# A two-layer hybrid backbone with expert routing: last layer's gate applied as the expert outputs leave PSUM, three-term sum on TensorE, and routing tables of 28 turns

## The reference

```python
p_group = softmax(t @ w_router_group); grp = argmax(p_group)          # 4 groups
top_p, top_j = top_k(softmax(logits of that group's 8 experts), 2)
gates = gate_group * top_p / top_p.sum()
f[token] = sum over its 2 experts e of  gate * ((silu(h @ w_gate[e]) * (h @ w_up[e])) @ w_down[e])
x = layer_norm(RES_ALPHA * x + g2 * f, ln2_g, ln2_b)                  # g2: one value per channel
```

## Time and profile before

| | us |
|---|---|
| median of 3 runs | 2641.17 |
| the profiled execution | 2639.44 |
| its span, first to last instruction | 2637.6 |
| TensorE matmul busy | 2328.2 (88%) |
| VectorE busy | 942.3 (36%) |
| ScalarE busy | 445.2 (17%) |
| GpSimd busy | 483.1 (18%) |

### The profile page before, as it was taken

How to read it: one execution, slowest core, us unless ns; L and a number is a source line. 1 busy time by engine, 2 the same in 40 slices (tenths; PEclk the granted TensorE clock), 3 DMA queues, 4 the chain that set the end, 5 groups by cost and what they waited for, 6 DMA issues and landing times. The chain is left out here.

```text
span 2637.6 us, 38801 instructions
## 1 busy us (share of the span) xinstructions
PE 2328.2 (88%) x14940; PEld 1620.1 (61%) x14940; DVE 942.3 (36%) x2263; ACT 445.2 (17%) x1115; POOL 483.1 (18%) x615
## 2 busy tenths in 40 slices
PE   5999779997399999999949987999399999999975
PEld 3999645654366666666629984555166666666642
DVE  1777736565511101110126665566611011101107
ACT  0011123331011111111111113232011111111111
POOL 0000013444011111111111111344011111111114
PEclk8999879998599999999979998999699999999987
DMA  9555430001588999999841113000289999999944
GB/s 356 186 169 161 146 112 16 18 24 49 204 321 353 387 397 390 386 392 403 324 162 68 49 49 130 16 25 17 110 347 388 394 385 394 385 386 381 372 189 192
DMA packets 131278, 608.71 MB, mean 231 GB/s; under 512 B 21376, under 2 KB 24448, under 8 KB 112752
## 3 DMA queue, kind: packets, MB, share of 16 engines
q1 hardware_dynamic: 113168, 569.61, 55.9%
q0 software_dynamic: 16864, 37.78, 3.8%
q10 hardware_dynamic: 1152, 0.03, 0.0%
HBM read 599.41 MB, written 42.04 MB: 243 GB/s over the span
## 5 line engine op out<-in xcount | busy, mean ns | idle before, releaser
L1966 PEld LDWEIGHTS gate_up<-room,w_gate_up 128*128 128x128 f32 x4608 | 520.8, 193 | 31.5 <-issue 31.5
L1966 PE MATMUL gate_up<-room,w_gate_up 128*128 128x128 f32 x4608 | 527.6, 277 | 3.1 <-DVE room L1873 3.1
L1975 PE MATMUL down<-w_down,room 128*128 128x512 f32 x576 | 256.8, 599 | 0.0
L1983 PE MATMUL gate_up_short<-w_gate_up,room 128*64 128x512 f32 x1152 | 255.1, 595 | 0.0
L1882 DVE TENSOR_TENSOR room<-room,gate_up 128x128 f32<-128x128 f32 x144 | 41.4, 288 | 597.4 <-ACT room L1901 597.4
L1885 DVE TENSOR_TENSOR room<-room,gate_up_short 128x256 f32<-128x256 f32 x36 | 15.2, 421 | 495.0 <-ACT room L1907 495.0
L1983 PEld LDWEIGHTS gate_up_short<-w_gate_up,room 128*64 128x64 f32 x1152 | 79.5, 137 | 171.2 <-issue 171.2
L1975 PEld LDWEIGHTS down<-w_down,room 128*128 128x128 f32 x576 | 106.5, 190 | 123.0 <-issue 120.5
L1593 POOL COPY rows_idx<-slot_token 128x1 int32 (+1 forms) x78 | 14.3, 183 | 791.6 <-PE rows_turned L1953 710.6
L1996 PE MATMUL down<-w_down,room 128*64 128x512 f32 x576 | 131.5, 598 | 11.9 <-ACT room L1909 11.9
L1404 PE MATMUL proj<-w_out,mixT 128*128 128x512 f32 x288 | 129.5, 592 | 0.0
(11 more groups left out here) (365 smaller groups left out, 3254.8 us busy)
## 6 DMA issues: line engine op xcount, KB each, us to landing
w_gate_up<-in_w_exp_gate SPq DMA_DIRECT2D x72, 2048.0 KB, 9.2
w_gate_up<-in_w_exp_up SPq DMA_DIRECT2D x72, 2048.0 KB, 13.7
w_down<-in_w_exp_down SPq DMA_DIRECT2D x72, 2048.0 KB, 12.5
ada_w<-in_w_ada SPq DMA_DIRECT2D x96, 512.0 KB, 4.8
h_rows<-h SPq DMA_DIRECT2D x18, 512.0 KB, 2.6
w_out<-in_w_out SPq DMA_DIRECT2D x2, 4096.0 KB, 13.2
w_in<-in_w_in SPq DMA_DIRECT2D x2, 3072.0 KB, 17.4
xn<-expert_rows SPq DMA_DIRECT2D x10, 512.0 KB, 4.0
```

The costliest lines, as they stand in the source:

```text
L1966: mm = nc.tensor.matmul(H[j % 2][:, o, :], wgu[0][:, o, k, j * P:(j + 1) * P], xT[0][:, k, :], start=k == 0, stop=k == KT - 1)
L1975: mm = nc.tensor.matmul(Y[:, h, :], hid[:, j, :], wd[0][:, j, h * 512:(h + 1) * 512], start=j == 0, stop=j == JT - 1)
L1983: mm = nc.tensor.matmul(Hs[c * HP:(c + 1) * HP, :, :], xT[1][:, k, :], wgu[1][:, :, k, c * 2 * P:(c + 1) * 2 * P], start=k == 0, stop=k == ...
```

## The change

It has four parts.

1. **Last stage.** TensorE sums three terms in PSUM: alpha times x (a diagonal matrix of alpha, two matmuls per tile, ahead of the wait for the landing) and the two experts' rows times their gates (four). Three sums of two banks take turns. VectorE takes the statistics straight from PSUM, centres from PSUM, and does the multiplication with one over the deviation and the addition of the bias of the tile before in between. ScalarE and GpSimd do no 1024-wide work. The load of g2 is gone, and the norm's vectors are fetched between tiles 0 and 1.
2. **Last layer's loop.** g2 is applied as the outputs leave PSUM, by VectorE in place of ScalarE's copies; g2 is loaded at the start of the block, by three DMAs on SP's queue. The first layer's loop is as before.
3. **Counts.** `total` sums over the tiles in PSUM (N matmuls of 32 columns), `before` is completed for earlier tiles by N-1 more matmuls; the running sums on VectorE are gone. The lines are turned by five matmuls of one column. Comparisons over 320 or 256 elements become integer shifts.
4. **Tables.** 28 columns in place of 44. Empty slots are marked through an offset of the digits. Names are made while VectorE waits for the counts. Table and place instructions are interleaved, so that `table_ready` comes behind the one-hot tables. The long one-hot table comes in two halves, and the short slots are decoded first.

```diff
-NTURNS = 44
-NOWHERE = float(1 << 20)
+NTURNS = 28
+NO_NAME = 4096.0
...
+                if last:
+                    sp.dma_start(g2[:, :], g.mods[l, 0:1, 5 * D:6 * D].to_broadcast([P, D])).then_inc(g2_in, 16)
+                    for h in range(2):
+                        sp.dma_start(g2_s[h * HP:(h + 1) * HP, :], ...).then_inc(g2_in, 16)
                 each_turn(sp, weights)
...
-                step(nc.vector.tensor_copy(tot[:, :, :], r(total)))
-                for t in range(1, N):
-                    step(tt(tot[:, t, :], tot[:, t, :], tot[:, t - 1, :], ALU.add))
-                    done()
...
+                v.wait_ge(counted, 1)
+                step(ts(count_i[:, 0, :], total, float(P - 1), None, ALU.add))
+                step(ts(count_i[:, 1, :], total, float(HP - 1), None, ALU.add))
+                done()
+                step(ts(count_i[:, :, :], count_i[:, :, :], 7, None, ALU.arith_shift_right))
+                done()
+                step(tt(parts[:, SHORT, :], count_i[:, 0, :], count_i[:, 1, :], ALU.subtract))
+                step(nc.vector.tensor_copy(parts[:, LONG, :], count_i[:, 1, :]))
...
+                step(tt(turn_hot[:, :, :, :], iota(K_IOTA, TC), wide(bits_f[0], TC), ALU.is_equal))
...
+                tt(short_hot[:, :, :, :], iota(K_IOTA, HP), wide(bits_s, HP), ALU.is_equal).then_inc(slots_hot, 1)
...
                 for i in range(2):
                     tt(name_hot[:, :, :, i, :], turn_hot[:, :, :, :], over(digit[:, i, :, :], TC), ALU.mult).then_inc(slots_hot, 1)
+                v.wait_ge(s.sem, listed)
+                nc.vector.tensor_copy(tab[:, :], tab_f[:, :]).then_inc(table_ready, 1)
+                for h in range(2):
+                    t = slice(h * (N // 2), (h + 1) * (N // 2))
+                    tt(long_hot[:, t, :, :], ..., ALU.is_equal).then_inc(slots_hot, 1)
...
                     turn_copy(i, 1)
+                    if last:
+                        v.wait_ge(yo_free[0], i + 1)
+                        for h in range(2):
+                            v.wait_ge(y_full, i * 2 + h + 3)
+                            tt(yo[:, h * 512:(h + 1) * 512], Y[:, h, :], g2[:, h * 512:(h + 1) * 512], ALU.mult).then_inc(y_done, 1)
                     v.wait_ge(silu_s_done, i + 1)
                     nc.vector.tensor_tensor(hid_s[:, :], silu_s[:, :], Hs[:, 1, :], ALU.mult).then_inc(hid_s_done, 1)
                     turn_copy(i + 1, 0)
+                    if last:
+                        v.wait_ge(yo_free[1], i + 1)
+                        v.wait_ge(ys_full, i + 2)
+                        tt(yo_s[:, :], Y[:, 0, :], g2_s[:, :], ALU.mult).then_inc(ys_done, 1)
...
-                nc.tensor.matmul(total, g.k[:, K_ONE:K_ONE + P], m, start=True, stop=True).then_inc(counted, 1)
-                nc.tensor.matmul(before, g.k[:, K_TRI:K_TRI + P], m, start=True, stop=True).then_inc(prefixed, 1)
+                ones = g.k[:, K_ONE:K_ONE + P]
+                for t in range(N):
+                    mm = nc.tensor.matmul(total, ones, both[:, t, :], start=t == 0, stop=t == N - 1)
+                mm.then_inc(counted, 1)
+                nc.tensor.matmul(before, g.k[:, K_TRI:K_TRI + P], both[:, :, :], start=True, stop=False)
+                for u in range(N - 1):
+                    mm = nc.tensor.matmul(before[:, u + 1:N, :], ones, across(both[:, u, :], N - 1 - u), start=False, stop=u == N - 2)
+                mm.then_inc(prefixed, 1)
+
+                pe.wait_ge(lines_ready, 2)
+                for j in range(5):
+                    mm = nc.tensor.matmul(col_ps[:, j:j + 1], line[:, j, :], g.k[:, K_ID:K_ID + 1], start=True, stop=True)
+                mm.then_inc(lines_turned, 1)
...
+                def moments(t):
                     v.wait_ge(summed, t + 1)
-                    nc.vector.tensor_tensor(y, S[t % 2][:, :, :].rearrange("p a n -> p (a n)"), g2[:, :], ALU.mult).then_inc(scaled, 1)
-                    v.wait_ge(scaled, t + 1)
-                    small(nc.vector.scalar_tensor_tensor(y, g.x[:, t, :], ALPHA, y, ALU.mult, ALU.add))
-                    done()
                     nc.vector.memset(spare[:, :], 0.0)
                     for j in range(2):
-                        small(nc.vector.bn_stats(stats[:, j, :], y[:, j * 512:(j + 1) * 512]))
+                        small(nc.vector.bn_stats(stats[:, j, :], S[t % NS][:, j, :]))
...
+                v.wait_ge(ln_in, 32)
+                moments(0)
+                centre(0)
+                for t in range(1, LT):
+                    moments(t)
+                    put(t - 1)
                     centre(t)
+                put(LT - 1)
...
                 for t in range(LT):
                     pe.wait_ge(diag_ready, t + 1)
+                    if t >= NS:
+                        pe.wait_ge(centred, t - NS + 1)
+                    for h in range(2):
+                        nc.tensor.matmul(S[t % NS][:, h, :], alpha[:, :], g.x[:, t, h * 512:(h + 1) * 512], start=True, stop=False)
                     pe.wait_ge(landed[t], 32)
                     for h in range(2):
                         for k, y in enumerate((ya, yb)):
-                            mm = nc.tensor.matmul(S[t % 2][:, h, :], diag[:, t, k, :], y[:, t, h * 512:(h + 1) * 512], start=k == 0, stop=k == 1)
+                            mm = nc.tensor.matmul(S[t % NS][:, h, :], diag[:, t, k, :], y[:, t, h * 512:(h + 1) * 512], start=False, stop=k == 1)
```

More of the change, by code:

```diff
@@ L1683, in _ @@
                 nc.vector.engine_nop().then_inc(exp_in, 1)
-                r = lambda x: x.rearrange("p (t e) -> p t e", t=N)
-                v.wait_ge(counted, 1)
-                step(nc.vector.tensor_copy(tot[:, :, :], r(total)))
+                for k in range(2):
+                    step(ts(names[:, :, k], g.ids[:, 0:N], 2.0, float(k), ALU.mult, ALU.add))
                 done()
-                for t in range(1, N):
-                    step(tt(tot[:, t, :], tot[:, t, :], tot[:, t - 1, :], ALU.add))
-                    done()
@@ L1692, in _ @@
[L1692 to L1699 removed]
+                step(ts(digit_i[:, 0, :, :], names[:, :, :], 6, None, ALU.arith_shift_right))
@@ L1728, in _ @@
                 src = ends_n
+                step(tt(half[:, :], src[:, SHORT, NE - 1:NE], src[:, LONG, NE - 1:NE], ALU.add))
                 step(nc.vector.tensor_copy(begin[:, :, 1:NE], src[:, :, 0:NE - 1]))
[L1730 to L1734, removed]
+                step(ts(gap0[:, :], src[:, LONG, NE - 1:NE], 2.0 * P, -float(P), ALU.mult, ALU.add))
@@ L1761, in _ @@
+                tt(line[:, 4, :], begin[:, SHORT, :], early[:, :], ALU.add).then_inc(lines_ready, 1)
+                v.wait_ge(prefixed, 1)
+                step(tt(short[:, :, :], before, across(limit[:, :], N), ALU.is_ge))
+                step(sts(val[:, :, :], across(begin[:, LONG, :], N), 2.0 * P, before, ALU.mult, ALU.add))
                 done()
-                step(sts(lift[:, :], src[:, LONG, :], -2.0 * P, lift[:, :], ALU.mult, ALU.add))
-                step(tt(diag[:, :, :], line[0:NE, :, :], across(g.k[0:NE, K_ID:K_ID + NE], 5), ALU.mult))
+                step(tt(short[:, :, :], short[:, :, :], across(lift[:, :], N), ALU.mult))
@@ L1764, in _ @@
                 done()
-                step(ts(lift[:, :], lift[:, :], float(P), None, ALU.add))
-                step(red(col[:, :], diag[:, :, :], AX, ALU.add))
+                step(tt(val[:, :, :], val[:, :, :], short[:, :, :], ALU.add))
+                for k in range(2):
+                    step(tt(picked[k][:, 0, :, :], chosen[k], before, ALU.mult))
                 done()
+                for k in range(2):
+                    step(tt(picked[k][:, 1, :, :], chosen[k], val[:, :, :], ALU.mult))
@@ L1768, in _ @@
+                v.wait_ge(lines_turned, 1)
+                step(nc.vector.tensor_copy(col[:, :], col_ps))
+                done()
+                for k in range(2):
+                    step(red(ranks[:, k, :, :], picked[k][:, :, :, :], AX, ALU.add))
+                placed = s.at()
                 iota0, iota1 = (g.k[0:NE, K_IOTA + j:K_IOTA + j + TC] for j in range(2))
@@ L1776, in _ @@
-                step(nc.vector.tensor_copy(tab_f[:, 4 * TC:4 * TC + 1], turns[0:1, :]))
+                step(tt(bits_f[0][:, :, :], bits_i[0][:, :, :], second_i[:, :, :], ALU.add))
+                step(sts(bits_s[:, :, :], second[:, :, :], -float(HP), bits_s[:, :, :], ALU.mult, ALU.add))
+                placed = s.at()
                 v.wait_ge(turns_listed, 1)
@@ L1901, in outputs @@
                         nc.scalar.activation(silu[:, j % 2, :], H[j % 2][:, 0, :], ACT.Silu).then_inc(silu_done, 1)
-                    act.wait_ge(yo_free[0], i + 1)
-                    for h in range(2):
-                        act.wait_ge(y_full, i * 2 + h + 3)
-                        nc.scalar.activation(yo[:, h * 512:(h + 1) * 512], Y[:, h, :], ACT.Copy).then_inc(y_done, 1)
+                    if not last:
+                        act.wait_ge(yo_free[0], i + 1)
```

(6 more changed lines are left out.)

254 lines of the change are left out of this document (110 added, 144 removed).

## The result

The changed kernel takes **2619.88 us** (median of 4 runs, 2618.28 to 2621.88), the kernel before 2641.17 (4 runs, 2637.63 to 2641.38): ratio 0.9924, interval 0.9912 to 0.9936. The profiled execution took 2621.88, its span is 2619.9, 17.7 shorter than before. The forecast was 2619, between 2606 and 2629.

A forecast was written before the change was run, and what follows sets the result against it. TensorE was taken to bound the expert loops, chains of VectorE instructions the routing and last stage. Terms -13.9, -7.0 and +0.1 sum to -20.8 from 2639.4, giving 2619 us, range 2606 to 2629.

The forecast's parts named there:

- the last stage: Final stage: six TensorE matmuls, 5.16 us per tile, replace VectorE's 6.73 us per tile as the limiter; gain 13.9 us.
- the loops' starts: Both expert loops begin earlier through the shorter routing, by 3.9 and 3.1 us, 7.0 us together.
- Last loop: Last expert loop: evictions moved to VectorE cost 0 in the 18 turns, and 0.1 us at the loop's end.
- Routing up to the places: Routing up to L1729: less VectorE work, slower TensorE totals; net -1.8 us in the first layer, -1.5 in the last.
- VectorE's price list: Routing: a VectorE instruction occupies about 1.04 ns per element and 0.07 us, plus 0.12 where the next waits for it.
- The totals: Routing counts: 10 (8) small fp32 matmuls at 0.165 us per weight load cost +2.4 us, in the last layer +1.9.
- From the places to the slots: Routing from L1729 to ready slots: 18.2 us against 26.7, -8.5; last layer 16.1 against 24.1, -8.0.
- The gather: Row fetch before each loop: falls into the weights' stream, takes 11.0 us instead of 4.6, costing 6.4 us more.
- (a): Before the loops: the row gather is not held up by weights, 12.8 us more gained, 2606 us; chance 15%.
- (b): Routing brings nothing: small fp32 matmuls at 0.25 us per load and the delayed gather eat 7 us; 2626 us; 17%.
- Rival (c): Last stage: six matmuls at half clock take 10.3 us per tile; 2654 us with the routing; chance 4%.
- Rival (d): Last stage: the sums start late or some tiles are slow; 2623 to 2630 us; chance 6%.

The follow-up runs named there:

- the stage alone: Kernel before with the whole new last stage and the last loop's evictions times g2, old routing kept: 2624.4 us, ratio 0.9943 against the kernel before.
- the routing alone: Changed kernel with the old last stage and ScalarE's evictions in both layers, new routing kept: 2635.53 us, ratio 0.9985 against the kernel before.

## Why the prediction was right, step by step

The sum was -20.8, the spans differ by 17.7 and the medians by 21.3. Two terms were off, with opposite signs: the last stage gave 1.9 more, the loops' starts 3.3 less. That the median (2619.88) came within 1 us of 2619 is in part luck: these errors partly cancel, and so does the draw of the two profiled executions, of which the last paragraph of this section tells.

**Last stage: -13.9 forecast, -15.8 measured.** The steps that carried it held. Six matmuls take 5.15 us a tile (5.16 forecast), VectorE waits for them, no instruction of 2.64 is left (the last kind measures 1.24), and from the last sum to the end it is 8.8 (8.9). What was mis-sized is the first sum: I left it where it was, 13.0 after the fetch, and it came at 11.3, halfway to the bound that I had given for an early rise of the clock (2575.3 in the time of the kernel before is 9.6 after the fetch). The early residual matmuls run at the lower clock, and tile 0's last two ones already at the higher:

```profile
2564.82 3.78 PE L2117 MATMUL sum_end<-x_res,alpha_diag_end 128*128 128x512 f32 x4 [12.79 <-ACT gate_diag_end L2073]
2569.95 2.07 PE L2121 MATMUL sum_end<-ya_end,gate_diag_end 128*128 128x512 f32 x2 [1.35 <-DMA yb_end<-expert_rows]
...
2574.02 1.02 PE L2121 MATMUL sum_end<-yb_end,gate_diag_end 128*128 128x512 f32 x2
```

Whether these early matmuls cause that is open: the run without them took 1.4 more, within the spread between runs, and its clock rose no later. An earlier start is worth little beyond this anyway, as the stage alone showed: at 9.0 the second tile's rows are the next wait.

**Last loop: 0 forecast, 0 measured.** A half took 0.69, as worked out; the turn is unchanged; the end +0.12 for the forecast +0.1. The last layer's first turn took 0.4 more, which was in no term.

**Routing up to the places.** VectorE's price list held: without the totals this part fell by 4.15 and 3.37 (4.2 and 3.4 by the steps). The totals themselves were mis-sized: +3.04 and +2.40 where I took +2.4 and +1.9. The cause is the load's spacing, 0.165 in the sum, between bounds of 0.11 and 0.25; 20 loads in 4.34 are 0.217. The stretch runs at half clock, and so does the row that gave 0.25; 0.11 is from a row at full clock, and the 0.165 lay too near to it.

**From the places to the slots.** -8.4 and -7.9 measured, -8.5 and -8.0 forecast. The first weights were issued 2.7 behind the end of the table's cast (687.48 + 0.20 to 690.41), for 2.8 forecast.

**The gather, the step I had named as the next wait.** +6.8 and +7.8 measured, +6.4 forecast from the one row of 11.0. The two runs that lift it show that it is the weights' stream: 11.6 behind gate, up and down, 7.1 with only gate's ahead, 4.6 with none ahead. The Trainium skill ("DMA: Bandwidth & Descriptors", "Queues, rings and completion order") has each DMA engine take turns between queues by whole packets; the three figures agree in direction, and the last layer's 12.3, 2.1 behind up's issue, shows that a single row was no upper bound. Together with the totals this makes 3.7 of the 7.0 us forecast for the loops' starts. That rivals (a) and (b) had named just these two prices was right; neither came about in full. (a) would have needed a gather of 4.6, and (b) a gain of nothing, where the routing alone shows 4.

**Rival (c), the last stage at half clock,** did not come about: the granted clock is 1.00 from 2575 until TensorE's last tile is done. The run with one sum, 0.76 with its pauses of some 4 us per tile, and the three rotating sums at 1.00 show that it is pauses which lower it here, not the rotation. **Rival (d)** fell with the 5.15 in every tile.

The medians differ by 21.3 where the spans differ by 17.7. The profiled execution of the kernel after was the slowest of its four (2621.88 against a median of 2619.88), and that of before was 1.7 below its median.

## What to carry to other kernels

When a chain of small instructions gets shorter, ask which transfer its end now runs into: here 14.6 of 18.4 us were lost because a small gather fell behind three large weight loads, and holding back only the loads that aren't wanted first brought 5 us; holding back all brought none. Taking over the work of a neighbour that slows an engine can be cheap, but by itself it was worth 3.2 us here: count the instructions of whichever engine is then the limiter. Price an unseen sequence by the row at the same clock, not by a value between rows at two clocks. A wait put on a full TensorE can cost more than its length, since the clock behind it may be the lower one.

## What the runs showed of the hardware

- The price of a gather of 128 rows from its issue to the first transposes: 4.5 to 4.8 us with no weights ahead or only the last 3 us of their stream beside it, 6.8 to 7.2 with one load of 2 MB issued 2.5 to 2.9 us ahead of it, 11.6 to 12.3 with three.
- A VectorE instruction of 1024 fp32 elements with two SBUF inputs took 2.64 beside GpSimd's additions, 1.23 without them, and 1.23 beside ScalarE's scaling.
- Twenty fp32 weight loads for ten 32-column matmuls took 4.34 us at half clock, whereas one matmul of 320 columns took 1.43: it is the number of loads and matmuls, not that of columns, which sets the time.
- A pause of 4.09 us in TensorE was followed by four records of 3.75 us in place of 1.88; the mean clock over the tile was 0.76. Behind one of 3.15 they took 1.96. Without pauses it stayed at 1.00 from the second tile to the eighth.
- A pause of 1.98 us once per turn of an otherwise full loop brought the clock of the next 5 us to 0.66 to 0.70 in every second turn and left it at 1.00 in the others.
- The first sum of the last stage varied between 9.0 and 12.8 us after the fetch from one kernel's profile to the next with the stage's code all but the same, and the stage's length by 2.5 at most.
